# Token load in two tiles, weight slab queued before the gate parameters, gate products after the first projection half

## The reference

```
for l in range(DEPTH):                                     # DEPTH = 2
    h = rmsnorm(x, attn_norm[l])                           # 256 x 1024
    (hq, hf, hi, hg, mq, mk, mv, mi, mf, mo, fq, fk, fv, ff) = split(h @ w_in[l])
    o_hg = hgrn2_mixer(hq, hf, hi, hg, lb_all[l], hgrn_norm[l])
    o_ml = mlstm_mixer(mq, mk, mv, mi, mf, mo, mlstm_conv[l], b_i[l], b_f[l], mlstm_norm[l])
    o_fx = fox_mixer(fq, fk, fv, ff, fox_b_f[l])
    x = x + concat(o_hg, o_ml, o_fx) @ w_out[l]
    h = rmsnorm(x, ffn_norm[l])
    x = x + (dense swiglu if l == 0 else top-2-of-8 expert swiglu)
return rmsnorm(x, final_norm)
```

## Time and profile before

| | us |
|---|---|
| median of 3 runs | 1554.12 |
| the three runs | 1554.05, 1554.12, 1557.11 |
| profiled execution | 1557.37 |
| its span in the trace | 1555.6 |
| PE busy | 1477.0 |
| DVE busy | 1165.6 |
| ACT busy | 952.6 |
| mean granted TensorE clock | 0.971 |

### The profile page before, as it was taken

One profiled execution on the slowest core, in us unless ns is written; L12 is line 12 of the kernel. 1 busy time (PEld: TensorE's weight loads), 2 busy tenths in 40 slices (PEclk: granted clock), 3 DMA queues, 4 the chain that ended last, 5 costly groups with the idle time before them and its releaser, 6 DMA issues.

```text
span 1555.6 us, 21085 instructions
## 1 busy us (share of the span) xinstructions
PE 1477.0 (95%) x8033; PEld 1257.2 (81%) x8033; DVE 1165.6 (75%) x921; ACT 952.6 (61%) x847; POOL 90.9 (6%) x103
## 2 busy tenths in 40 slices
PE   6999799997999979999999999999999999999993
PEld 6988499997988658888888888888888888888882
DVE  4883354544686258888888888888888888889884
ACT  4454244443545227777777777777777777777772
POOL 4221000000031120000000000000000000000001
PEclk8999999999899969999999999999999999999997
DMA  8431695543333169999999999999999999999983
GB/s 262 163 109 55 210 317 190 190 138 133 109 113 112 49 229 349 388 376 375 396 367 374 395 387 370 395 369 370 394 379 366 394 387 373 394 370 365 395 339 108
DMA packets 211785, 449.19 MB, mean 289 GB/s; under 512 B 12884, under 2 KB 37016, under 8 KB 211736
## 3 DMA queue, kind: packets, MB, share of 16 engines
q1 hardware_dynamic: 210584, 444.31, 78.5%
q0 software_dynamic: 1152, 4.19, 0.7%
HBM read 433.80 MB, written 14.68 MB: 288 GB/s over the span
## 4 chain that ended last, share of the span: by engine, by line
PE 89%; DVE 5%; ACT 2%; issue 1%; DMA 1%; SPq 1%; POOL 0%; DVEq 0%; POOLq 0%; ACTq 0%
PE bank L1371 26%; PE bank L1373 26%; PE bank L1372 26%; PE bank L1594 2%; PE bank L1581 2%; PE bank L1678 2%; ACT winh L711 1%; PE bank L1425 1%; DVE QD L995 1%; DVE low L1223 1%; DMA ring<-in_w_in_dram 1%; DVE winl L963 1%; DVE SC L1004 0%; ACT XN L679 0%; PE bank L1665 0%
## 5 line engine op out<-in xcount | busy, mean ns | idle before, releaser
L1223 DVE TENSOR_TENSOR low<-raw,high 128x2048 fp32r<-128x2048 f32 x336 | 769.1, 2298 | 112.2 <-ACT high L880 112.2
L880 ACT CAST high<-raw 128x2048 fp32r<-128x2048 f32 x336 | 644.6, 1919 | 178.0 <-PE bank L1373 178.0
L1371 PE MATMUL bank<-high,xeh 128*128 128x512 f32 x896 | 353.5, 395 | 0.0
L1373 PE MATMUL bank<-high,xel 128*128 128x512 f32 x896 | 349.5, 390 | 0.0
L1372 PE MATMUL bank<-low,xeh 128*128 128x512 f32 x896 | 348.8, 389 | 0.0
L1373 PEld LDWEIGHTS bank<-high,xel 128*128 128x128 f32 x896 | 168.2, 188 | 35.8
L1372 PEld LDWEIGHTS bank<-low,xeh 128*128 128x128 f32 x896 | 168.4, 188 | 33.7
L1371 PEld LDWEIGHTS bank<-high,xeh 128*128 128x128 f32 x896 | 168.3, 188 | 33.7 <-issue 0.2
L1371 PE MATMUL bank<-high,hdh 128*128 128x512 f32 x448 | 175.0, 391 | 0.0
L1373 PE MATMUL bank<-high,hdl 128*128 128x512 f32 x448 | 174.4, 389 | 0.0
L1372 PE MATMUL bank<-low,hdh 128*128 128x512 f32 x448 | 174.3, 389 | 0.0
(11 more groups left out here) (281 smaller groups left out, 1945.0 us busy)
## 6 DMA issues: line engine op xcount, KB each, us to landing
raw<-in_moe_w_gate_dram SPq DMA_DIRECT2D x112, 1024.0 KB, 7.7
raw<-in_moe_w_up_dram SPq DMA_DIRECT2D x112, 1024.0 KB, 8.2
raw<-in_moe_w_down_dram SPq DMA_DIRECT2D x112, 1024.0 KB, 7.7
ring<-in_w_in_dram SPq DMA_DIRECT2D x10, 2048.0 KB
dring<-in_dense_w_gate_dram SPq DMA_DIRECT2D x5, 2048.0 KB
dring<-in_dense_w_up_dram SPq DMA_DIRECT2D x5, 2048.0 KB
dring<-in_dense_w_down_dram SPq DMA_DIRECT2D x5, 2048.0 KB
ring<-in_w_in_dram SPq DMA_DIRECT2D x8, 1024.0 KB
```

The lines of the kernel that those rows point to most:

```text
L880: act.copy(high[:, q % SPLIT, :], raw[:, q % RAW, :]).then_inc(s_hi, 1)
L1223: dve.tensor_tensor(low[:, q % SPLIT, :], raw[:, q % RAW, :], high[:, q % SPLIT, :].bitcast(F32), ALU.subtract).then_inc(s_lo, 1)
L1371: pe.matmul(o, xh, wh, start=first, stop=False)
L1373: return pe.matmul(o, xl, wh, start=False, stop=last)
```

## The change

X is loaded as two transfers, one for each token tile, with a semaphore each, and ACT's two square sums wait each for its own. On SP, slab 0 comes directly behind the gain rows; behind it come layer 0's gate parameters, columns first, then slab 1, layer 1's gate parameters, the head gains and the router. On ACT, in layer 0 as in layer 1, the weights of half 0 are rounded before hT. On PE, in both layers, the gate products stand between projection halves 0 and 1. On ACT the three gate steps stand behind the logarithms of half 0, and on DVE all gate steps stand behind `weights_low` of half 2 and the two steps on half 0 (L1090, L1091).

```diff
-        s_x = sem("x_loaded")
+        s_x = [sem(f"x_loaded{t}") for t in range(T)]
...
-            sp.dma_start(X[:, :, :], x[0].rearrange("(t p) d -> p t d", p=P)).then_inc(s_x, 16)
+            for t in range(T):
+                sp.dma_start(X[:, t, :], x[0, t * P:(t + 1) * P, :]).then_inc(s_x[t], 16)
...
-            for l in range(DEPTH):
-                for src, c0, n in ((mlstm_b_i, 0, NH), (mlstm_b_f, NH, NH), (fox_b_f, 2 * NH, NFH)):
-                    sp.dma_start(GB[:, l, c0:c0 + n], src[l:l + 1, :].to_broadcast([P, n])).then_inc(s_par, 16)
+            def gate_params(l):
+
                 wi = w_in[l].rearrange("(k p) n -> p k n", p=P)
                 sp.dma_start(WG[:, l, :, 0:2 * NH], wi[:, :, MI0:MI0 + 2 * NH]).then_inc(s_par, 16)
                 sp.dma_start(WG[:, l, :, 2 * NH:16], wi[:, :, FF0:FF0 + NFH]).then_inc(s_par, 16)
+                for src, c0, n in ((mlstm_b_i, 0, NH), (mlstm_b_f, NH, NH), (fox_b_f, 2 * NH, NFH)):
+                    sp.dma_start(GB[:, l, c0:c0 + n], src[l:l + 1, :].to_broadcast([P, n])).then_inc(s_par, 16)
...
                     if l == 0 and i == 0:
+                        gate_params(0)
+                    if l == 0 and i == 1:
+                        gate_params(1)
                         for ll in range(DEPTH):
...
             def square_sums(i):
-                if i == 0:
-                    act.wait_ge(s_x, 16)
-                elif i < 2 * DEPTH:
+                if 0 < i < 2 * DEPTH:
                     act.wait_ge(s_res, 4 * i)
                 for t in range(T):
+                    if i == 0:
+                        act.wait_ge(s_x[t], 16)
...
-                if l:
-                    weights_high(l, 0)
+                weights_high(l, 0)
                 turned_high(l, hTh, 8 * l)
-                if not l:
-                    weights_high(l, 0)
                 weights_high(l, 1)
 
-                act.wait_ge(s_gv, l + 1)
-                log1p_exp_neg_abs(GA[:, 3, :, :], GA[:, 0, :, :], s_ga, 3 * l)
                 evacuate(l, 0)
                 act.wait_ge(s_pe, NHALF * l + 1)
                 h1 = 3 * l
                 log1p_exp_neg_abs(TMP, FZ, s_h1, h1)
+                act.wait_ge(s_gv, l + 1)
+                log1p_exp_neg_abs(GA[:, 3, :, :], GA[:, 0, :, :], s_ga, 3 * l)
                 evacuate(l, 1)
...
                 weights_low(l, 1)
+                weights_low(l, 2)
+
+                dve.wait_ge(s_h1, 3 * l + 3)
+                dve.wait_ge(s_pe, NHALF * l + 1)
+                h2 = 2 * l
+                dve.scalar_tensor_tensor(out=LS, in0=FZ, scalar=0.0, in1=TMP, op0=ALU.min, op1=ALU.subtract).then_inc(s_h2, 1)
+                dve.scalar_tensor_tensor(out=NK, in0=FZ, scalar=0.0, in1=TMP, op0=ALU.max, op1=ALU.add).then_inc(s_h2, 1)
 
                 dve.wait_ge(s_par, NPAR)
                 dve.wait_ge(s_gp, l + 1)
...
-                weights_low(l, 2)
-
-                dve.wait_ge(s_h1, 3 * l + 3)
-                dve.wait_ge(s_pe, NHALF * l + 1)
-                h2 = 2 * l
-                dve.scalar_tensor_tensor(out=LS, in0=FZ, scalar=0.0, in1=TMP, op0=ALU.min, op1=ALU.subtract).then_inc(s_h2, 1)
-                dve.scalar_tensor_tensor(out=NK, in0=FZ, scalar=0.0, in1=TMP, op0=ALU.max, op1=ALU.add).then_inc(s_h2, 1)
...
                 turn(2 * l)
 
+                project(l, 0)
+
                 pe.wait_ge(s_par, NPAR)
-                pe.wait_ge(s_hT, 4 * (2 * l) + 4)
                 for t in range(T):
                     for k in range(KD):
                         ins = pe.matmul(ps[7][:, t * 16:(t + 1) * 16], hT[:, k, t * P:(t + 1) * P], WG[:, l, k, :],
                                         start=(k == 0), stop=(k == KD - 1))
                 ins.then_inc(s_gp, 1)
-                project(l, 0)
                 project(l, 1)
```

## The result

| | before | changed |
|---|---|---|
| median of 10 runs, us | 1554.89 (1554.05 to 1557.85) | 1558.35 (1557.03 to 1562.46) |
| profiled execution, us | 1557.37 | 1557.43 |
| ratio to before | | 1.0018 (95% interval 1.0010 to 1.0027) |

The two medians differ by 3.5 us; the ratio with its interval puts the loss at 2.8 us (1.6 to 4.2), just under the 0.2% that counted as "same" in the forecast. +2.5 us was forecast, as a median of 1556.6. The two profiled executions are level, since the one of before is a long one among its runs and the changed one a short one among its own. They serve to see the steps, not to read off the sum.

The account below looks back on a forecast made before the run. PE, busy for 95% of the span, was taken as the bound. Layer 0 +0.5, layer 1 -1.0 and clock falls +3.0 gave +2.5 us on a median of 1554.1: 1556.6 us, range 1551.5 to 1560.0.

Parts of the forecast that it names:

- Start of half 0, layer 0: Layer 0's projection half 0 starts on PE at 19.3 us instead of 22.3, 3.0 us earlier.
- L: Moment slab 0, with layer 0's first projection weights, lands: taken as 12.0 us, between 11.3 and 12.9.
- L + 7.3: Layer 0: half 0 starts 7.3 us after slab 0 lands, after roundings of weights and hT, hTl and winl.
- Price of the products: Gate products between halves 0 and 1 cost PE 3.5 us per layer, bounds 0 and 7.0.
- The clock behind them: Behind the gate products the clock falls to 0.50 for 3.4 us, costing 1.5 us per layer, 3.0 in both.
- The rival in which the clock holds: No clock fall between the halves: sum -0.5 us, time 1553.6; chance 20%.
- The rival in which the low stretch doubles: Clock falls early in the gate products, low stretch twice 3.4 us: about 3 us per layer, sum +5.5; chance 20%.
- Layer 0 in sum: Layer 0's half 1 copied out 0.5 us later before the clock fall's 1.5 us, near 38.4 us with it.
- Layer 1 in sum: Layer 1: half 0 starts 4.5 us earlier, products cost 3.5: 1.0 us earlier, before the clock fall's 1.5 us.
- the 0.5 us that I named for this: Layer 1's half 0: 0.5 us given back if the clock needs 5.2 us to rise instead of 3.9.
- Cover for the parameters: Layer 0's gate parameters land by about 20 us, PE needs them at about 27: 7 us of cover, no cost.
- What moves half 1 moves the end.: In each layer, what shifts the copying out of projection half 1 shifts the kernel's end, since later steps hang on it.

Follow-up runs that it names:

- strewn: Changed kernel with its 16 gate products set into the first eight steps of projection half 1, two behind each dense triple, both layers: 1556.71 us, ratio 1.0001.
- the doubled set: Changed kernel with every gate product made twice: 1570.84 us, ratio 1.0096.

## Why the prediction was right

- **Start of half 0, layer 0.** L was put at 12.0 and measured 12.38, the start at 19.3 and 19.83. The gain was 2.5 us instead of 3.0. The step "L + 7.3" held (7.45). Two slips of 0.1 us in it change nothing: 1.9 + 2.3 + 0.1 is 4.3, and 11.3 + 7.3 is 18.6.
- **Price of the products.** 3.5 us forecast, 3.48 on the chain.
- **The clock behind them.** Falls of 3.4 us in both layers, as forecast. That the piece causes them is shown by the traces: 13 of 13 in one piece, none of eight strewn or in two. With both layers strewn the time went down as well: 0.9995 (0.9986 to 1.0003; its other edit, hT first, gave nothing in time when made alone, 1.0021) against 1.0020 (1.0011 to 1.0029) for the changed kernel on the same chip. In layer 1 alone it did not (0.9999 against 0.9998, and 161.81 against 161.78 us for the layer's mixer in the traces). So the 1.5 us per layer is what a fall costs at its place, and not in each layer what it adds to the end. The rival in which the clock holds, fell. With it fell the reading by which PE's busy share keeps the clock up, which one could take from the Trainium skill, "TensorE: Matmul & The Clock Gate", under "What's actually happening": the rule speaks of how busy PE has been, and PE was busy for 4.00 of 4.00 us in the stretches before, in and behind the fall to a mean of 0.58. The rival in which the low stretch doubles did not come for one set of products; the doubled set shows that it is real for a longer piece.
- **Layer 0 in sum.** +0.5 and +1.5 forecast, so 38.4; 38.97 measured, mostly the later landing.
- **Layer 1 in sum.** -1.0 and +1.5 forecast, so +0.5; +1.0 measured. The start came 4.5 us earlier as put down. The clock rose 5.0 us after it (at 400.6) instead of the 3.9 us that I chose; the 0.5 us that I named for this and left out of the sum is the difference.
- **Cover for the parameters.** The forecast had slab 1 issued at about 7 us and 7 us of cover. SP's timeline in the changed kernel:

```profile
4.58 1.70 SPq L431 DMA_DIRECT2D WG<-in_w_in_dram  x1
6.32 2.78 SPq L432 DMA_DIRECT2D WG<-in_w_in_dram  x1
9.14 2.64 SPq L434 DMA_DIRECT2D GB<-in_mlstm_b_i_dram  x1
...
12.78 0.47 SPq L457 DMA_DIRECT2D ring<-in_w_in_dram  x1
...
13.89 4.05 SPq L432 DMA_DIRECT2D WG<-in_w_in_dram  x1
...
21.32 0.43 SPq L434 DMA_DIRECT2D GB<-in_fox_b_f_dram  x1
```

With slab 0 issued ahead of them, the issues of gate columns, 0.43 and 0.58 us before, took 1.70, 2.78 and up to 4.05, and that of a bias 2.64 in place of 0.36 to 0.93. Slab 1 was issued at 12.8, the last parameter at 21.3, and the products began at 28.0 without a wait. The conclusion held with less room; the step was mis-sized, and in the two runs with layer 0's products in front PE waited for the parameters (until 15.35 us in the first).
- **"What moves half 1 moves the end."** This is the step that failed in part. From the copy of half 1 to the first residual add of layer 0 there are 129.1 us in the kernel before, with a fall at 68 to 72 us, and 127.6 in the changed one, without. In layer 1 before, there are 130.3 us, against 127.6. The stretches of the kernel before show two falls there:

```profile
444.00:448.00 4.00, 4.00 (x28) 3.78 (x27) 3.75 (x2) 1.38 (x3) 2.19 (x1) 0.58 0.10 16
471.00:475.00 4.00, 4.00 (x21) 4.00 (x22) 3.47 (x3) 2.33 (x3) 1.56 (x1) 0.57 0.18 65
```

The changed kernel has none of the three:

```profile
68.00:72.00 4.00, 4.00 (x33) 3.23 (x33) 2.94 (x6) 3.55 (x4) 0.09 (x1) 1.00 0.00 0
...
444.00:448.00 4.00, 4.00 (x33) 3.36 (x33) 2.95 (x5) 3.42 (x4) 0.47 (x1) 1.00 0.00 0
471.00:475.00 4.00, 4.00 (x38) 3.88 (x35) 3.37 (x3) 2.86 (x5) 1.03 (x1) 1.00 0.32 114
```

A head with a fall can miss one that the other meets further down. So +2.6 and +1.0 us at the heads became 0 in the two profiled executions.

The other traces bear this out for layer 1. In the six with a fall at half 1 and the products made once, 127.6 us pass from the copy of half 1 to the next residual add, and there is no fall at 444 us. In the five with the products strewn or in two pieces it is 129.0 to 129.1 us, and all five have the fall at 444. From the first residual add to the next these eleven take 161.6 to 162.0 us, wherever their fall is; the kernel before takes 163.3 with its two. In layer 0 the rule is looser. A fall near 68 to 74 us stands in five of the eight traces without a fall at half 1, and in none of the six with one, but two of these six have a fall at 94 to 100 us. The kernel with layer 1 alone in one piece has the layer 0 of the kernel before, and no fall there. And with layer 1's products in their old place, as in the kernel before, the clock fell neither at half 1 nor at 444. So the head does not decide it alone.

What stays open: the ratio puts the loss at 2.8 us where the two profiled executions show none, and the other executions behind the medians have no trace. The runs point to layer 0. Layer 1 alone in one piece shows no cost (0.9998), and undoing layer 1 gains nothing (1.0018, with the 0.9 us that it brings along), though each of these intervals is 1.4 us wide to either side. The traces say the same: the first residual add of layer 0 comes at 165.45, 165.66 and 163.29 us in the three kernels with the old layer 0, and at 166.54, 166.42 and 167.11 in the three with the changed one; the other forms of layer 0 lie between 164.06 (strewn) and 167.19 (X as one transfer). No run changed layer 0 alone. That the sum of the forecast came out so near is in part luck: the two heads lost 3.6 us where 2.5 was forecast, and a part was given back further down. The forecast time, 1556.6, also stood on a median of three runs; that of ten is 0.8 us higher.

## What to carry to other kernels

Moving work behind the start of a dense stretch is not free when PE has no gap there: compare the start gained with the price at the new place, and add what the granted clock does. The gate products kept PE busy in the profile and yet let the clock fall; set between dense matmuls two at a time they cost only their own time at that place. Whether it is their 16 columns or their plain float32 that lets it fall, no run here tells apart. When a queue's order is changed, the issuing engine's times change too, and engines whose steps were ordered around the old place may now hold up others. One trace of each kernel is not enough to add up what falls of the clock cost: they lie elsewhere from one to the next.

## What the runs showed of the hardware that was not expected

- A fall of the clock at one place can replace one further on: 32.69 us of head with a fall at 444 us, 34.21 without it, and 161.81 and 161.78 us for the whole mixer. In layer 1, five of five traces with strewn or halved products fell at 444, and none of the seven with a fall at half 1.
- SP's issues take longer with slabs issued ahead of them: 4.05 us for one that took 0.58.
- The profile gives a clock of 1.00 before the first change it records, and the pitch contradicts it: in the run with layer 0's products in front, all 32 entries took 6.98 us, which is the pitch of 0.218 us at 0.50, although the stretch is given as 1.00:

```profile
15.35:22.33 6.98, 6.98 (x33) 6.98 (x34) 6.91 (x10) 2.70 (x3) 6.30 (x11) 1.00 0.91 289
```

  In the kernel before, 20 of them took 0.11 us each in the same place. The kernel with layer 1 alone in one piece has the same layer 0 as that one, and all 32 took 0.218 us:

```profile
15.05 6.98 PE L1507 MATMUL bank<-WG,hT 128*128 128x16 f32 x32 [0.87 <-DVE hT L949]
```

  So which of the two an execution gets is not the kernel's doing. For the same reason the mean granted clocks of two executions are not to be compared: the changed kernel ran its first dense matmuls at the pitch of 0.21 us up to 25.2 us, and its trace gives 1.00 there.
